# Two output chunks accumulated side by side in the delta rule's last tail, earlier head norms, and five reordered waits, in a two-layer encoder on one core

## What the kernel computes

```python
for layer in range(2):
    h = rms_norm(x, norm_mix[layer])
    x = x + (even_mixer(h, ...) if layer == 0 else odd_mixer(h, ...))
    x = x + memory_cross_attention(rms_norm(x, ...), rms_norm(mem, ...), ...)
    x = x + squared_relu_mlp(rms_norm(x, ...), w1, w2)
# even_mixer: q, k, v = silu(conv(h @ w)); g, beta from 32 gate columns
#   o = delta_rule(q, k, v, g, beta) + flip(delta_rule(flipped))      8 heads of 128
#   y_dn = rms_norm_per_head(o) * gain * silu(gate);  y_sc = b * conv(c * u)
#   return concat([y_dn, y_sc]) @ w_out                               2048 x 2048
```

## Time and profile before

| | us |
|---|---|
| median of 3 runs | 2813.24 (2809.95 to 2817.38) |
| the profiled execution | 2808.52 |
| its span in the trace | 2806.4 |
| TensorE busy | 2743.1 (98%) |
| VectorE busy | 1541.5 (55%) |
| ScalarE busy | 1312.9 (47%) |
| GpSimd busy | 119.7 (4%) |
| mean granted TensorE clock | 0.994 |

### The profile page before, as it was taken

The page is one execution under the profiler, slowest core; times in us unless marked ns, Lnnn a source line. Parts: engine busy times, 40 slices in busy tenths (PEclk is TensorE's granted clock), DMA queues, the critical chain, the costliest instruction groups (busy, mean ns, idle before and its releaser), DMA issues.

```text
span 2806.4 us, 44803 instructions
## 1 busy us (share of the span) xinstructions
PE 2743.1 (98%) x18220; PEld 2407.3 (86%) x18220; DVE 1541.5 (55%) x2039; ACT 1312.9 (47%) x1789; POOL 119.7 (4%) x167
## 2 busy tenths in 40 slices
PE   8999999999999999999999998899999999999999
PEld 8999998887888888888898898688878888888887
DVE  5555566665555555555544556655655555555554
ACT  4544444555544535445344444334655445354453
POOL 0000043000000000000000000350000000000000
PEclk9999999999999999999999999999999999999999
DMA  7454510543555555555534553003435555545553
GB/s 278 156 192 167 173 39 32 210 173 127 180 195 190 186 195 190 189 191 195 195 136 177 191 194 140 2 2 127 174 122 188 200 185 191 195 180 196 194 186 144
DMA packets 67798, 461.68 MB, mean 165 GB/s; under 512 B 7023, under 2 KB 10223, under 8 KB 13084
## 3 DMA queue, kind: packets, MB, share of 16 engines
q1 hardware_dynamic: 63824, 449.47, 44.7%
q10 hardware_dynamic: 3500, 5.21, 0.5%
q0 software_dynamic: 288, 4.19, 0.4%
HBM read 456.73 MB, written 5.27 MB: 165 GB/s over the span
## 4 chain that ended last, share of the span: by engine, by line
PE 92%; DVE 4%; ACT 2%; issue 1%; DMA 0%; ACTq 0%; POOL 0%; DVEq 0%; POOLq 0%
PE bank L419 17%; PE bank L400 13%; PE bank L402 13%; PE bank L401 13%; PE bank L421 9%; PE bank L442 6%; PE bank L444 6%; PE bank L443 5%; PE bank L1149 1%; PE bank L1122 1%; PE bank L335 1%; DVE split_lo L351 1%; ACT split_hi L344 0%; DVE hT L592 0%; PE bank L503 0%
## 5 line engine op out<-in xcount | busy, mean ns | idle before, releaser
L351 DVE TENSOR_TENSOR split_lo<-raw,split_hi 128x1024 fp32r<-128x1024 f32 x840 | 1020.7, 1224 | 967.1 <-ACT split_hi L344 966.7
L344 ACT ACTIVATE split_hi<-raw 128x1024 fp32r<-128x1024 f32 x840 | 881.7, 1059 | 1164.7 <-PE bank L402 578.1
L419 PE MATMUL bank<-hT,split_hi 128*128 128x512 f32 x2048 | 717.7, 396 | 1.6 <-DVE hT L592 1.5
L421 PE MATMUL bank<-hT,split_lo 128*128 128x256 f32 x2048 | 572.8, 280 | 0.0
L419 PEld LDWEIGHTS bank<-hT,split_hi 128*128 128x128 f32 x2048 | 384.1, 188 | 94.6 <-issue 2.3
L400 PE MATMUL bank<-split_hi,u_hi 128*128 128x512 f32 x1152 | 449.5, 390 | 0.0
L402 PE MATMUL bank<-split_hi,u_lo 128*128 128x512 f32 x1152 | 448.4, 389 | 0.0
L401 PE MATMUL bank<-split_lo,u_hi 128*128 128x512 f32 x1152 | 448.3, 389 | 0.0
L421 PEld LDWEIGHTS bank<-hT,split_lo 128*128 128x128 f32 x2048 | 386.3, 189 | 0.1
L442 PE MATMUL bank<-hT,split_hi 128*128 128x256 f32 x1328 | 378.0, 285 | 3.1 <-DVE hT L592 1.8
L443 PE MATMUL bank<-hT,split_hi 128*128 128x256 f32 x1328 | 376.9, 284 | 0.0
(11 more groups left out here) (456 smaller groups left out, 2291.6 us busy)
## 6 DMA issues: line engine op xcount, KB each, us to landing
raw<-in_stream SPq DMA_DIRECT2D x420, 1024.0 KB, 4.8
work<-in_mem POOLq DMA_DIRECT2D x2, 2048.0 KB, 9.2
bias_rows<-bias_line SPq DMA_DIRECT2D x1, 3072.0 KB, 13.1
hwork<-bias_rows ACTq DMA_DIRECT2D x2, 1536.0 KB, 9.5
x<-in_x SPq DMA_DIRECT2D x1, 2048.0 KB, 9.1
out<-x SPq DMA_DIRECT2D x4, 512.0 KB, 5.2
rwork<-in_wide ACTq DMA_DIRECT2D x1, 1280.0 KB, 13.6
const<-in_masks SPq DMA_DIRECT2D x1, 1129.5 KB, 13.5
```

What stands on the lines that cost most here:

```text
L344: nc.scalar.activation(split_hi[:, u % SPLIT], raw[:, b % RAW, (u % 2) * UNIT:(u % 2 + 1) * UNIT], ACT.Copy).then_inc(s_hi, 1)
L351: nc.vector.tensor_tensor(split_lo[:, u % SPLIT], raw[:, b % RAW, (u % 2) * UNIT:(u % 2 + 1) * UNIT], f32(split_hi[:, u % SPLIT]), SUB).th ...
L419: nc.tensor.matmul(out[:, :], lhsT=w_hi[:, cols], rhs=hT[:, k].rearrange("p two s -> p (two s)"), start=k == 0, stop=False)
L421: m = nc.tensor.matmul(out[:, S:2 * S], lhsT=w_lo[:, cols], rhs=hT_hi[:, k, :], start=False, stop=k == KD - 1)
```

## The change

It touches these places:

- Gate columns: the two transposes move into chunk 2, behind its fourth unit; ScalarE does the copy of chunk 2, the SiLU of chunk 1 and two further splits ahead of and within `gates`.
- Cross attention, either layer: the values' evacuation and the transposed copies move ahead of one split on ScalarE and on VectorE; four fills go in behind the transposes; `xa_o` waits for each half where its k-tiles need it.
- Window attention: `pe_keep_busy` 9 becomes 19. RWKV: 16 fills go in ahead of the first inversion, behind a wait for the first masked copy.
- `ev_out`: chunks 0 and 1 share their eight k-units in halves (chunk 0 units 0 to 3, chunk 1 units 0 to 3, chunk 0 units 4 to 7, chunk 1 units 4 to 7), and the stream's units are packed in that order. Units 0 and 1 of chunk 0 stand in slots 20 and 23 of the last inversion; units 2 and 3 and unit 0 of chunk 1 in its tail. The fills there go. The last tail uses banks 6 and 7.
- The splits of the convolution output move into the last inversion, into an own tile `scT`. Heads 0 to 5 are normed and gated there in place; heads 6 and 7 afterwards.

```diff
+def shared_unit(name, c, u):
+    half = UNITS_OF[name] // 2
+    return (2 * (u // half) + c) * half + u % half
...
+            def row_unit(self, name, c, u, lhsT):
+                acc = self.banks(c)
+                w_hi, w_lo = self.unit(shared_unit(name, c, u))
+                ... (the six products of row_chunk for k-tiles 2u and 2u + 1)
+                m.then_inc(s_used, 1)
...
 pe_cross_mix
+            taken_of(pe, f"xa_q{l}", 0)
+            pe_fill(chunk_banks(f"xa_o{l}", 0)[0][0], 4)
             pe.wait_ge(s_xpt_a, 2 * l + 2)
...
-            pe.wait_ge(s_xoT, 2 * l + 2)
+                k_ready = None if c else lambda k: pe.wait_ge(s_xoT, 2 * l + 1 + k // 2)   # xa_o
...
 act_out_cross and dve_out_cross
-            hi_upto(act, chunk_done(f"mem_v{l}", 0) + AHEAD)    # moved behind the copies L873; lo_upto behind L955
...
 pe_even
-            qkv.column_chunk(1)
-            pe.wait_ge(s_abv, 1) ... two transposes
+            qkv.column_chunk(1)
+            qkv.column_chunk(2, after_unit=turn_gates)          # the same, at u == 3
...
+                    if hp + 1 == DN_GROUPS and slot in EARLY_SLOTS:          # (20, 23)
+                        pe.wait_ge(s_os, DN_GROUPS - 1)
+                        out_unit(0, EARLY_SLOTS.index(slot))
+                    elif slot in (20, 23) and hp + 1 < DN_GROUPS:
                         pe_fill(bank[7], 4 if slot == 20 else 5)
...
             for step in range(5):
                 pe_delta_tail(pe, DN_GROUPS - 1, step)
-                if step < 4:
-                    pe_fill(bank[7], 4)
+                if step == 0:
+                    turn_heads(0)
+                    turn_heads(1)
+                elif step < 4:
+                    out_unit(*((0, 2), (0, 3), (1, 0))[step - 1])
+            turn_heads(2)
+            for u in range(1, 4):
+                out_unit(1, u)
+            turn_heads(3)
+            for c in range(2):
+                for u in range(4, 8):
+                    out_unit(c, u)
...
 act_even, last inversion (SC_SLOTS = (0, 1, 3, 5))
+                    if hp + 1 == DN_GROUPS and slot in SC_SLOTS:
+                        ... hi of two scT tiles (the fourth waits for s_o of group 2)
+                    if hp + 1 == DN_GROUPS and slot >= 6 and slot % 2 == 0:
+                        hi_upto(act, starts["ev_out"][1] + (slot - 4) // 2)
+                    if hp + 1 == DN_GROUPS and slot == 7:
+                        act.wait_ge(s_oe, 1)
+                        ... root of heads 0 to 5
...
 dve_even, last inversion
+                    if hp + 1 == DN_GROUPS and slot - 1 in SC_SLOTS:
+                        ... lo of two scT tiles
+                    if hp + 1 == DN_GROUPS and slot >= 7 and slot % 2 == 1:
+                        lo_upto(dve, starts["ev_out"][1] + (slot - 5) // 2)
+                    slot 6: mean squares of heads 0 to 5; slot 9: scale_heads(0, 6); slot 10: gate_heads(0, 6)
...
-                    pe_keep_busy(chunk_banks("od_rw", 2)[0][0], 9)
+                    pe_keep_busy(chunk_banks("od_rw", 2)[0][0], 19)
...
             pe_rwkv_pairs(pe, 0, 1)
+            pe.wait_ge(s_rMAT, 1)
+            pe_fill(bank[0], 16)
```

More of the change, by code:

```diff
@@ L169, in build @@
         mwork = place("mwork", [P, 4 * XA_H * S], offset=mem_at)
+        scT = place("scT", [P, 8, 2, S], F32R, offset=mem_at)
         mem_kT = [place(f"mem_kT{l}", [P, XA_H, S]) for l in range(2)]
@@ L453, in chunk_done @@
         def chunk_done(name, c):
+            if name in SHARED and c == 0:
+                return starts[name][1] + 3 * UNITS_OF[name] // 2
             return starts[name][1] + UNITS_OF[name] * (c + 1)
@@ L1307, in pe_even, with out_tile, out_unit @@
                 Gemm(pe, "ev_sc").column_chunk(c, after_unit=lambda u, c=c: pe_delta_head(pe, c, u))
+            out = Gemm(pe, "ev_out")
+            def out_tile(k, t):
+                if k < 8:
+                    at = SC_AT[k // 2] + k % 2
+                    return scT[:, at, 0, t * P:(t + 1) * P], scT[:, at, 1, t * P:(t + 1) * P]
+                at = DN_TILE[k // 2 - 4]
+                return hT_tile(at.start + k % 2 * (at.step or 1), t)
+            def out_unit(c, u):
+                pe.wait_ge(s_yT, u + 1)
+                out.row_unit("ev_out", c, u, out_tile)
             for hp in range(DN_GROUPS):
@@ new lines, in act_even, with take_heads @@
+            u = starts["ev_out"][1]
+            hi_upto(act, u + 5)
+            def take_heads(b):
+                act.wait_ge(s_yt, b + 1)
+                nc.scalar.activation(hT_hi[:, DN_TILE[b], :], aux[b % 2][:, :].rearrange("p (h s) -> p h s", s=S),
+                                     ACT.Copy).then_inc(s_ysp, 1)
+            act_delta_tail(act, DN_GROUPS - 1, (0,))
+            take_heads(0)
+            act_delta_tail(act, DN_GROUPS - 1, (1,))
+            take_heads(1)
+            hi_upto(act, u + 7)
@@ L1761, in between @@
                             dve_inv_first(dve, hp + 1, dn_inv[(hp + 1) % 2], d)
-                    if hp + 1 == DN_GROUPS and 7 <= slot < 7 + AHEAD:
-                        lo_upto(dve, starts["ev_out"][1] + slot - 6)
-                dve_inv(dve, hp, dn_inv[hp % 2], between)
+                    if hp + 1 == DN_GROUPS and slot - 1 in SC_SLOTS:
+                        b = SC_SLOTS.index(slot - 1)
+                        dve.wait_ge(s_ysp, b + 1)
+                        nc.vector.tensor_tensor(scT[:, SC_AT[b]:SC_AT[b] + 2, 1, :], yscT[:, 2 * b:2 * b + 2, :],
+                                                f32(scT[:, SC_AT[b]:SC_AT[b] + 2, 0, :]), SUB).then_inc(s_yT, 1)
@@ L2894 @@
             got = row_units(matrices[name])
+        if name in SHARED:
+            per = UNITS_OF[name]
+            own = got.copy()
+            for c in range(2):
+                for i in range(per):
+                    got[shared_unit(name, c, i)] = own[per * c + i]
         stream[u:u + len(got)] = got
```

165 lines of the change are left out of this document (99 added, 66 removed).

## The result

| | before | after |
|---|---|---|
| median of the runs on one chip, us | 2813.59 (4 runs, 2809.95 to 2817.38) | 2793.48 (4 runs, 2789.1 to 2794.7) |
| ratio after/before, 95% interval | | 0.9928 [0.9915, 0.9941] |
| profiled execution / its span, us | 2808.5 / 2806.4 | 2794.7 / 2792.8 |
| mean granted clock of that execution | 0.994 | 0.994 |
| TensorE at half clock ahead of the program's end, us | 30.7 | 34.1 |

The change is 20.1 us faster; 25.8 were forecast. The last two lines of the table are the surprise: the mean clock is the same, and TensorE spends a little more time at half clock than before, at other places. The two profiled executions differ by 13.8 only: before's, at 2808.5, was quicker than all four of its timed runs, after's was the slowest of its four.

The account below looks back on a forecast made before the run. TensorE was taken as the bound (92% of the chain of waits), each wait costing its length plus half a following half-clock stretch. 6.9 + 8.4 + 3.6 + 1.6 + 5.3 = 25.8 us gave 2787.4; range 2781 to 2798.

Parts of the forecast that it names:

- the tail: Last inversion and delta tail: fills and waits of 6.8 us go, VectorE hold-ups cost 1.4; 5.3 taken from the layout.
- Gates, 6.9: Gate columns: 2.7 us wait at the transposes, 2.9 of half clock behind it and 1.3 wait in chunk 3 go.
- Cross attention, 4.2 a layer: Each layer: 1.1 us off the wait, 1.8 from the clock, 1.4 ahead of `xa_o`, less 0.1; 8.4 for both.
- with the split (about 1 us) moved behind, both copy chains end near 655.6: Cross attention: ScalarE's and VectorE's copies end near 655.6 instead of 656.6, taking 1.1 us off the 1.9 wait.
- Window attention, 3.6: Nineteen products fill the wait and hold the clock: 1.0 us from transposes, 2.5 from scores; 3.6 taken, bounds 0 and 5.2.
- RWKV, 1.6: First RWKV inversion: sixteen fills fit the 3.85 us wait; with the clock up, the group behind costs 1.89 instead of 3.49.
- The hold-ups inside the inversion: Last inversion: third lo part starts level 4's second direction 0.6 us late; fourth with mean squares delays level 4's subtraction 0.8.
- rival 4: Slower: interleaved tail loses the clock from slot 20 to chunk 1's end; at worst 2787 + 55 = 2842 us; chance 0.02.
- in the new order almost none is left: Last inversion and tail: almost none of the several waits of 0.3 to 1.2 us remains, an argument against the clock falling.
- The five stretches at half clock gone: Sign of being right: half-clock stretches of 6.9, 3.5 (both cross attentions), 10.3 and 3.6 us behind the targeted waits disappear.
- VectorE's contention with GpSimd: Last inversion: three of four lo parts run beside GpSimd, 0.2 us each, counted as nothing; by the skill, 5.3 becomes 4.0.

Follow-up runs that it names:

- after_again: The changed kernel run once more, unchanged, for a second trace and more times: 2794.27 us, ratio 0.9941 to the kernel before.
- tail_only: Kernel before with only the shared output chunks, earlier splits and earlier norms, the five gaps outside the delta tail left as before: 2812.88 us, ratio 1.0012.
- split_behind: Changed kernel with the last split ahead of the memory values put really behind the transposed copies, on ScalarE and VectorE: 2788.74 us, ratio 0.9917.
- hold: Changed kernel with 4, 3 and 1 fills in TensorE's waits in slots 12, 15 and 16 of the last inversion: 2788.76 us, ratio 0.9915.
- clock_fills: `lo_odd` plus four products ahead of layer 1's first product and fills before the first two transposes L2125 and in the first RWKV inversion: 2790.35 us, 0.9909.
- lo_odd: Changed kernel with VectorE's four `scT` lo parts moved to slots 1, 3, 5 and 7 of the last inversion, mean squares in slot 5: 2790.86 us, 0.9937.
- no_tail: Kernel before with only the five gaps outside the delta tail (gates, two cross attentions, window attention, RWKV): 2794.22 us, ratio 0.9945.
- all_fixes: `clock_fills` and `split_behind` together: 2789.53 us, ratio 0.9917 to the kernel before.
- best_no_tail: Changed kernel with the order of `split_behind` and the added fills of `clock_fills`, but delta tail, output chunks and norms as before: 2805.47 us, ratio 0.998.

## Why the prediction was right, and where it was wrong

The time lay inside the range, and 6.1 us above the forecast. That says little of the tail: its 5.3 could be missing whole and the time would still have been inside (2792.7). `after_again`, on another chip, gained 15.8 (2810.1 to 2794.3), so the 20.1 is itself good to a few us. By its terms:

- **Gates, 6.9: right.** The trace has 7.0, no wait at the transposes or in chunk 3, and the clock at 1.00 over 78 to 85. The price of a fall read from two splits was sound for that execution; in `tail_only`, with the same wait, the stretch was 3.4 instead of 6.8.
- **Cross attention, 4.2 a layer: 3.4 and 3.4.** Clock and `xa_o` came as laid out: L820 takes 3.69 for the 3.6 forecast, and `xa_o` starts behind it without a wait. The step that failed is "with the split (about 1 us) moved behind, both copy chains end near 655.6". I read the line that moved and not the bound of the loop in front, which left it nothing to do. `split_behind` gives the 1.1.
- **Window attention, 3.6: right in its place.** The trace has 3.6 (from 9.5 to 13.1), and the first two groups of scores take 2.83, where 2.9 was the mark:

```profile
1703.01 8.37 PE L338 MATMUL bank<-const 128*128 128x256 f32 x38
1711.66 1.09 PE L2075 MATMUL bank<-const,work 128*128 128x128 f32 x8 [0.28 <-ACT work L2173]
1713.58 2.83 PE L2087 MATMUL bank<-work 128*128 128x256 f32 x12 [0.83 <-ACT work L2173]
...
1721.80 1.54 PE L2125 MATMUL bank<-const,work 128*128 128x128 f32 x6 [1.11 <-DVE work L2272]
```

  But the clock then fell at 1719.0, ahead of the wait of 1.11 in the fence, and 1.2 went back. In the time of before that is 1732.1, some 2.5 us behind the end of its stretch of 10.3.
- **RWKV, 1.6: right in its place, then overdrawn.** The sixteen fills end as the inversion starts (L343 from 1771.46 for 3.84, L1150 at 1775.38), and up to 1790 the trace gains 1.6. Then the clock fell behind this wait, and again at 1807.7 with no wait ahead of it, and 3.5 went back:

```profile
1790.56 1.05 PE L1150 MATMUL bank<-rwork,work 64*64 64x64 f32 x16 [1.13 <-DVE rwork L1236]
```

- **Tail, 5.3: 0.9.** The layout was right to 0.6 us, as `hold` shows with 4.7. (What goes adds up to 6.7 by its parts, not 6.8.) The hold-ups inside the inversion, put at 0.6 and 0.8, came out as waits of 0.92, 0.62 and 0.21 where before had 0.54: 1.2 more than before, for 1.4. What failed is the sentence under rival 4 that "in the new order almost none is left", with its reason that the inversion of before "ran at 1.00" with several waits of 0.3 to 1.2. I had 1.4 us of VectorE hold-ups in my own layout and priced them at their length. They cost about that and then 3.4 to 3.8 more, because the clock fell for 10.2: 3.4 between executions of the same code (`clock_fills` and `lo_odd`), 3.8 between the changed kernel and `hold`. The mechanism is rival 4's, some slots ahead of the place named there and for 10.2 us; I had priced it only at 34 us of loss and more, at a chance of 0.02.
- **"The five stretches at half clock gone": wrong as a whole.** Three are gone, those of the gates and of the two cross attentions. In the window attention and in the RWKV part one came back further on, some 13 and 16 us behind the start of the old one. Three more are new (459.5, 1408.4 and 1807.8), and the sum went from 30.7 to 34.1. A gap that is closed took its stretch with it, but many short waits are left, and a wait that passed without a fall before can have one now: at 1408.4 the clock fell behind a wait of 1.8 that the kernel before has as well. The prediction took each fall as the price of one wait, and that step failed.

The profiled pair gives 13.6 of 25.8: 4.4 missing in the tail, 1.6 in the cross attentions, 1.2 in the window attention, 3.5 in RWKV, 1.5 at layer 1's input product (sum 12.2). The medians give 20.1, because the profiled execution of before was quicker than its timed runs and that of after was the slowest of its four.

VectorE's contention with GpSimd was counted at nothing, and that was too little. VectorE's lo parts in the last inversion of the changed kernel (the third is above, 1.00):

```profile
448.31 1.09 DVE L1861 TENSOR_TENSOR scT<-work,scT 128x512 fp32r<-128x512 f32 x1
...
450.00 0.65 DVE L1861 TENSOR_TENSOR scT<-work,scT 128x512 fp32r<-128x512 f32 x1
...
459.91 0.65 DVE L1861 TENSOR_TENSOR scT<-work,scT 128x512 fp32r<-128x512 f32 x1
```

The first lies beside GpSimd's level masks (L1139, the L1111 of before) and takes 0.44 more than the two that have GpSimd at rest; the third lies beside its scaled values (L1952, the L1844 of before) and takes 0.35 more. That is about twice the 0.2 taken from L1831, and the third is on TensorE's path: the wait behind it is 0.92, and 0.6 had been laid out. GpSimd's instruction beside each of them took 0.45 longer as well (1.17 for 0.72, 1.06 for 0.61). By the Trainium skill (SBUF — State Buffer, SBUF: two separate sides) the engine that starts first has the lock for its whole instruction and the other is blocked. The rows fit that: the two lo parts began 0.18 and 0.17 behind the start of a GpSimd instruction of 0.72 and 0.61, so 0.54 and 0.44 of it were left, and they took 0.44 and 0.35 more.

## What to carry to other kernels

Where TensorE is the bound and its list has short waits, price a wait of even 0.6 to 1.1 us at its length and, as a second term with a chance of its own, at half of a stretch at half clock behind it; put fills into the waits that remain before counting a layout's gain. When a closed gap was followed by a fall, look for the next wait behind it, which may take it over; and look at stretches of small products without any wait, where the clock fell in nine traces here. When instructions are moved to another place in an engine's list, read in the new trace what now stands ahead of the awaited one (`lo_odd`). When a call like "split up to unit n" is moved, work out the bound that the calls ahead of it reach, for the moved line may do nothing.

## What the runs showed of the hardware

- **The clock differs from one execution to the next of the same program.** The 17 runs of the kernel before beside `no_tail` took 2802.5 to 2815.6 us, and their mean granted clock goes with it: the five at 0.991 and 0.992 all took over 2811 us, the five quickest were at 0.994 to 0.997. The last inversion lost the clock in `clock_fills` and kept it in `lo_odd` and `all_fixes`, with the same code up to there. A gain that lies in the clock is a shift of odds, and one trace shows one draw. What decides a draw is open.
- **The MLP's turns have two paces.** With no stretch at half clock and no wait, a turn takes either about 175.9 or about 177.6 us, in the same program:

```
turns, us       layer 0 (the last is longer)      layer 1
before          177.6  177.6  175.9  184.1        176.1  177.7  175.8  177.7
after           175.9  176.0  177.8  185.8        175.9  177.5  177.6  176.1
hold            177.7  175.9  177.6  185.7        175.9  177.5  175.9  176.1
best_no_tail    175.9  177.7  177.7  184.0        175.9  182.9  180.7  181.0
```

  In a slow turn each of the four column chunks takes 22.6 instead of 22.2; the row chunks take 21.8 in either. In the thirteen traces without a pause the eight turns sum to 1412.5 to 1418.5 us, so 6 us come and go with it. In the profiled pair they are alike (1414.6 and 1414.7). Its cause is open, and none of the experiments went at it.
- **A pause for nothing shown.** The same loop ran with three pauses of 3.2 to 3.6 us at one place in the program and with none a few instructions on: 13.6 us by two small products, for a reason that no run shows. A kernel that comes out many us off a neighbour deserves a look at `issue` before any theory on its edit.
